# Layer 1's input projection: 41 more weight units in three fp32r products, 60 low parts made ahead in layer 0's FFN and read back from DRAM

## The reference, cut to what matters

```
xn = rmsnorm(x); proj = xn @ w_in                       # 2048 -> 8272 columns: u, q, k, v, index q/k/w, gates gl
q, k = rope(rmsnorm(.)); y_att = top-k sparse attention(q, k, v, index scores)
y_ssm = S5 scan(u) (complex states);  y_ssm = gelu(y_ssm); y_ssm *= sigmoid(y_ssm @ w_glu)
gates = sigmoid(gl)
x += (gates0 * (y_ssm @ w_branch0) + gates1 * (y_att @ w_branch1)) @ w_out
x += (silu(hn @ w_gate) * (hn @ w_up)) @ w_down         # hn = rmsnorm(x), width 5632
```

## Time and profile before

| | |
|---|---|
| median of 3 runs | 3007.73 us (3007.71 to 3008.23) |
| the profiled execution | 3008.11 us |
| its span | 3006.3 us |
| TensorE busy | 2963.9 us, 99% |
| VectorE busy | 1965.7 us, 65% |
| ScalarE busy | 1247.4 us, 41% |
| GpSimd busy | 254.5 us, 8% |
| granted TensorE clock | 1.00 of full speed |
| DMA | 546.45 MB, mean 182 GB/s |

### The profile page before, as it was taken

How to read it: one execution, slowest core, us unless ns; L and a number is a source line. 1 busy time by engine, 2 the same in 40 slices (tenths; PEclk the granted TensorE clock), 3 DMA queues, 4 the chain that set the end, 5 groups by cost and what they waited for, 6 DMA issues and landing times. The chain is left out here.

```text
span 3006.3 us, 58601 instructions
## 1 busy us (share of the span) xinstructions
PE 2963.9 (99%) x23480; PEld 2838.4 (94%) x23480; DVE 1965.7 (65%) x3145; ACT 1247.4 (41%) x1745; POOL 254.5 (8%) x239
## 2 busy tenths in 40 slices
PE   8999999999999999999999999999999999999999
PEld 7988888999999999999999887889999999999999
DVE  7669898577665545655576698985776555465653
ACT  4443234444545333334344423344444543333332
POOL 4420001300000000000034200013000000000000
PEclk9999999999999999999999999999999999999999
DMA  7547444655555655556555574456555555555564
GB/s 264 171 154 201 146 147 163 226 176 178 198 182 182 200 169 179 183 182 205 187 201 172 159 199 131 153 172 216 180 185 190 183 182 199 168 182 181 181 207 137
DMA packets 150623, 546.45 MB, mean 182 GB/s; under 512 B 19872, under 2 KB 25632, under 8 KB 149952
## 3 DMA queue, kind: packets, MB, share of 16 engines
q1 hardware_dynamic: 137728, 507.40, 50.4%
q0 software_dynamic: 12096, 35.67, 4.7%
q10 hardware_dynamic: 640, 1.16, 0.1%
HBM read 536.95 MB, written 7.21 MB: 181 GB/s over the span
## 5 line engine op out<-in xcount | busy, mean ns | idle before, releaser
L1847 DVE TENSOR_TENSOR w_ffn_low<-ring_ffn,w_ffn_high 128x1024 fp32r<-128x1024 f32 (+1 forms) x480 | 638.9, 1332 | 456.4 <-ACT w_ffn_high L1351 456.4
L1351 ACT ACTIVATE w_ffn_high<-ring_ffn 128x1024 fp32r<-128x1024 f32 (+1 forms) x480 | 548.1, 1142 | 641.6 <-PE main L1064 640.6
L1062 PE MATMUL main<-x_ffn_high,w_ffn_high 128*128 128x264 f32 x2816 | 791.7, 281 | 0.0
L1063 PE MATMUL main<-x_ffn_low,w_ffn_high 128*128 128x264 f32 x2816 | 791.3, 281 | 0.0
L1064 PE MATMUL main<-x_ffn_high,w_ffn_low 128*128 128x264 f32 x2816 | 791.3, 281 | 0.0
L1062 PEld LDWEIGHTS main<-x_ffn_high,w_ffn_high 128*128 128x128 f32 x2816 | 526.6, 187 | 0.1
L1063 PEld LDWEIGHTS main<-x_ffn_low,w_ffn_high 128*128 128x128 f32 x2816 | 526.6, 187 | 0.1
L1064 PEld LDWEIGHTS main<-x_ffn_high,w_ffn_low 128*128 128x128 f32 x2816 | 526.6, 187 | 0.0
L1062 PE MATMUL main<-hidden_high,w_ffn_high 128*128 128x264 f32 x1408 | 395.6, 281 | 0.0
L1063 PE MATMUL main<-hidden_low,w_ffn_high 128*128 128x264 f32 x1408 | 395.6, 281 | 0.0
L1064 PE MATMUL main<-hidden_high,w_ffn_low 128*128 128x264 f32 x1408 | 395.6, 281 | 0.0
(11 more groups left out here) (375 smaller groups left out, 4785.3 us busy)
## 6 DMA issues: line engine op xcount, KB each, us to landing
ring_ffn<-in_w_up SPq DMA_DIRECT2D x352, 512.0 KB, 3.3
ring<-in_w_in SPq DMA_DIRECT2D x260, 512.0 KB, 3.4
ring_ffn<-in_w_down SPq DMA_DIRECT2D x128, 704.0 KB, 4.1
ring<-in_w_br SPq DMA_DIRECT2D x64, 512.0 KB, 3.4
ring<-in_w_out SPq DMA_DIRECT2D x64, 512.0 KB, 3.3
w_low<-in_w_in POOLq DMA_DIRECT2D x20, 512.0 KB, 7.0
ring<-in_w_glu SPq DMA_DIRECT2D x16, 512.0 KB, 3.3
out_x<-x SPq DMA_DIRECT2D x7, 528.0 KB, 5.9
```

Source lines behind the costliest of these rows:

```text
L1062: mm(out, wfh[:, slot, w], high[:, kk, :], start=kk == 0, stop=False)
L1063: mm(out, wfh[:, slot, w], low[:, kk, :], start=False, stop=False)
L1351: af(wfh[:, s, 0:cols], ring_ffn[:, s, 0:cols], ACT.Copy).then_inc(high_ready, 1)
L1847: tt(wfl[:, s, 0:cols], ring_ffn[:, s, 0:cols], wfh[:, s, 0:cols].bitcast(F32), ALU.subtract).then_inc(low_ready, 1)
```

## The change

In layer 1 41 more units of `w_in` are split: 116 of 130 in place of 75, all from 65 on. 52 of them have their low part made by VectorE as before (`HALVED`), 4 by the accumulating DMA (`DRAWN`), and 60 get it from DRAM (`STORED`): there ScalarE still makes the high part in layer 1, while VectorE does nothing. These 60 low parts are made in layer 0's FFN, two in each of the 30 bodies (`beside`, after steps 2 and 6): GpSimd loads the raw unit of layer 1, ScalarE copies it to its fp32r rounding in `between` (the padding between the 264-wide rows of the FFN's moving operands), VectorE subtracts in place, GpSimd stores the result. Odd ones are held in two halves, the first of which lies over the last half slot of `ring`, so `prefetch(5)` waits until all odd ones are stored. In layer 1 SyncE loads a stored low part into `w_low` after its high part is made. The gates lie in `xn`'s place, the high parts get other places, x is reloaded 28 units later, the merged parts change places, and the units stand elsewhere: four more in the count stage, one fewer before the norms' spread, three in place of six in `s5_in(1)`. Layer 0's mixer is as it was.

```diff
-X_AT = 112
+X_AT = (112, 140)
+DRAWN = [60, 63, 66, 69]
+STORED = [67, 68, *(u for u in range(70, 132) if u not in (75, 79, 83, 87))]
+HALVED = [*range(10, 56), 59, 65, 75, 79, 83, 87, *range(G_GLU, G_END)]
+LOW_AT = {0: 59, 6: 65, 15: 75, 18: 79, 22: 83, 25: 87}
+HIGH_PLACE = {59: "b0", 60: "w2", 63: "w3", 65: "b0", 66: "w2", 67: "w1", 68: "w0", 69: "w3",
+              **{u: ("q0", "q1", "w2", "w3")[u % 4] for u in range(102, 118)},
+              **{u: ("e", "q0", "q1")[(u - 118) % 3] for u in range(118, 131)}, 131: "v"}
...
                 finish(i, s, up, half, n0, seq0)
+                if beside and s in (2, 6):
+                    beside(i, first_body, s // 4)
...
+            if layer and 56 <= u < G_GLU:
+                return max((n + 1 for n in (*HALVED, *STORED, *DRAWN) if n < u and high_place(n) == high_place(u)), default=0)
...
+                    def load_low(u):
+                        if layer and u in STORED:
+                            sp.wait_ge(unit_high, highs_by(layer, u))
+                            sp.dma_start(wlow[:, u % 6, :].bitcast(F32), d["lows"][STORED.index(u)]).then_inc(stored_low_in[u % 4], 16)
...
+                    def load_with_x(u):
+                        load(u)
+                        k = u - X_AT[layer]
+                        if 0 <= k < NT:
+                            sp.dma_start(x[:, k, :], (o["x"] if layer else d["x"])[:, k, :]).then_inc(x_in, 16)
+                        if u - 2 < 118:
+                            load_low(u - 2)
+                        if u - 3 >= 118:
+                            load_low(u - 3)
...
                                 for u in (4, 5, 2, 3, 6, 7):
+                                    if u == 5:
+                                        sp.wait_ge(next_low_out[1], 32 * (len(STORED) // 2))
                                     prefetch(u)
...
-                    for f in range(28, 44):
-                        for c in range(2):
-                            w_in_unit(f, c)
-                            pe.wait_ge(count_ready, 2 * (f - 28) + c + 1)
-                            mm(side[0][:, 0:2], same_seq_r[:], n_over_r[:], start=True, stop=True).then_inc(total_ready, 1)
+                    for n in range(32):
+                        fill(1)
+                        pe.wait_ge(count_ready, n + 1)
+                        mm(side[0][:, 0:2], same_seq_r[:], n_over_r[:], start=True, stop=True).then_inc(total_ready, 1)
+                        if layer and n in (12, 18, 24, 30):
+                            fill(1)
...
-                    fill(2)
+                    fill(1 if layer else 2)
...
-                    s5_in(1, 50, 6)
+                    s5_in(1, None, 3 if layer else 6)
...
+                            if layer:
+                                highs_to(2 * f + 5 if f < 57 else min(2 * f + 4, 130))
...
+                    if layer:
+                        act.wait_ge(v_out, 16)
+                        highs_to(131)
+                        act.wait_ge(units, 130)
                     gelu(0)
...
+                    def next_layer_high(i, first_body, odd):
+                        act.wait_ge(next_raw_in[odd], i * (16 + 16 * odd) + (16 + 16 * odd) * (first_body + 1))
+                        act.wait_ge(coming_low, i * 2 + (2 * first_body + odd + 1))
+                        if odd:
+                            af(between[:, 0:16, :], odd_first[:].bitcast(F32).rearrange("p (c n) -> p c n", n=32), ACT.Copy)
+                            af(between[:, 16:32, :], odd_last[:].bitcast(F32).rearrange("p (c n) -> p c n", n=32), ACT.Copy)\
+                                .then_inc(coming_high, 1)
+                        else:
+                            af(between, even_part[:].bitcast(F32).rearrange("p (c n) -> p c n", n=32), ACT.Copy).then_inc(coming_high, 1)
...
+                    def next_layer_low(i, first_body, odd):
+                        dve.wait_ge(coming_high, i * 2 + (2 * first_body + odd + 1))
+                        if odd:
+                            for part, at in ((odd_first, 0), (odd_last, 16)):
+                                raw = part[:].rearrange("p (c n) -> p c n", n=32)
+                                op = tt(raw, raw.bitcast(F32), between[:, at:at + 16, :].bitcast(F32), ALU.subtract)
+                            op.then_inc(coming_low, 1)
...
+                    if layer == 0:
+                        pool.wait_ge(units, UN_FFN)
+                        for n in range(2):
+                            next_raw(n)
+                        for n in range(len(STORED)):
+                            pool.wait_ge(coming_low, n + 2)
+                            store_low(n)
+                            pool.wait_ge(next_low_out[n % 2], (16 + 16 * (n % 2)) * (n // 2 + 1))
+                            if n + 2 < len(STORED):
+                                next_raw(n + 2)
```

More of the change, by code:

```diff
@@ L368, in high_free, with highs_by, lows_by, stored_by @@
             return u - 3
-        def highs_by(u):
-            return sum(n <= u for n in SPLIT)
-        def lows_by(u):
-            return sum(n <= u for n in SPLIT)
+        def highs_by(layer, u):
+            return sum(n <= u for n in high_made(layer))
+        def lows_by(layer, u):
+            return sum(n <= u for n in low_made(layer))
+        def stored_by(u):
+            return 16 * sum(n <= u and n % 4 == u % 4 for n in STORED)
         main = [ctx.enter_context(nc.psum_tensor(f"main{i}", [P, 512], F32)) for i in range(4)]
@@ L550, in build @@
         for layer in range(DEPTH):
+            made_high, made_low, added = high_made(layer), low_made(layer), low_by_adding(layer)
             with nc.Block() as block:
@@ L1094, in highs_to @@
                             next_high += 1
-                            if u not in SPLIT and u not in ADDED:
+                            if u not in made_high and u not in added:
                                 continue
-                            raw, high, low = unit_w(u)
+                            raw, high, low = unit_w(layer, u)
                             act.wait_ge(u_in[u % 6], landed(u))
-                            if high_free(u):
-                                act.wait_ge(units, high_free(u))
-                            if u in ADDED:
+                            if high_free(layer, u):
+                                act.wait_ge(units, high_free(layer, u))
+                            if u in added:
                                 af(high, raw, ACT.Copy)
@@ L1401, in lows_to @@
                             next_low += 1
-                            if u not in SPLIT:
+                            if u not in made_low:
                                 continue
-                            raw, high, low = unit_w(u)
-                            dve.wait_ge(unit_high, highs_by(u))
+                            raw, high, low = unit_w(layer, u)
+                            dve.wait_ge(unit_high, highs_by(layer, u))
                             tt(low, raw, high.bitcast(F32), ALU.subtract).then_inc(unit_low, 1)
@@ L1986, in _ @@
                     for b in range(3):
-                        pool.wait_ge(units, 2 * 63 + 2 * b)
+                        pool.wait_ge(units, 131 if layer and b else 2 * 63 + 2 * b)
                         gather_keys(b)
```

219 lines of the change are left out of this document (149 added, 70 removed).

## The result

The changed kernel takes 3022.71 us (median of 4 runs, 3018.09 to 3026.65) against 3007.72 for the kernel before on the same chip (3007.16 to 3008.23): a ratio of 1.005, 95% interval [1.0038, 1.0063]. It is 15 us slower, where 7 us faster was forecast and 3015 was the upper end of the range. The profiled execution took 3026.65 us, its span is 3024.8 us at a mean granted clock of 0.997; the kernel before had 1.000.

The account below looks back on a forecast made before the run. Bound: TensorE (busy 2963.9 of 3006.3 us), but with VectorE in layer 1's count and attention stages. Sum: -9.5 (`w_glu` earlier) + 2.7 (end of layer 0) = -6.8 on 3008.11, 3001.3, or 3001.0 for the median; range 2989 to 3015.

Parts of the forecast that it names:

- Stored low parts in layer 1: Layer 1's reads from DRAM: budget 8.0 us, 5.0 for units 118 to 130, landing 3.4 us, so no cost.
- From `w_glu` on the units are as before: Layer 1 from `w_glu` to its end: units unchanged, so no further difference in time.
- Count stage: Layer 1's count stage: 36 units in place of 32, 115.3 us, ending 4.4 us later.
- First softmax step: VectorE's first softmax step in layer 1: at 1896.4, 8.5 us earlier.
- Attention stage: Layer 1, first softmax step to scan's end: VectorE still needs 94.0 us, so the scan ends 8.5 us earlier.
- `w_glu`: Start of layer 1's `w_glu`: at 2002.9, 9.5 us earlier.
- Layer 0's FFN: Making two low parts in each body of layer 0's FFN fits the engines' and DMA's slack: cost nothing.
- End of layer 0: Unit 5's load waits for the last stores, landing after 4 to 7 us: cost 1.0 to 4.0, 2.7 taken.
- C: Rival: stored low parts late in layer 1's units 70 to 107, 32 units wait 1.0 us each: 3033, chance 0.08.
- A: Rival: TensorE stays the bound all through, gaining 27 less 2.7 us: 2984, chance 0.08.
- B: Rival: little left; count stage +5 or late second scan in layer 1, 4 us at layer's end: 3007, chance 0.24.
- D: Rival: layer 0's FFN stalls, 0.5 us in each of 30 bodies: 3016, chance 0.08.

Follow-up runs that it names:

- e10: Changed kernel without loads of stored low parts (high part taken twice, output wrong) and with e6's places for the merged values: 3001.62 us, ratio 0.9985.
- e6: Changed kernel with layer 1's merged values elsewhere: high part where the low part lay, low part in the free place: 3014.73 us.
- e4: Changed kernel without layer 1's loads of stored low parts; the high part is taken a second time instead, output differs: 3013.04 us.
- e1: The changed kernel run once more, unaltered, to see its spread: 3020.95 us (3018.63 to 3024.63).
- e3: Changed kernel with layer 1 as changed, but layer 0's FFN makes only two low parts, which every read takes: 3021.95 us.
- e8: Changed kernel with 58 stored low parts, not 60: units 67 and 68 stay fp32, none made in layer 0's last FFN body: 3025.56 us.
- e9: Changed kernel with TensorE held once, 1.68 us, between the first up and first down half of layer 1's FFN: 3021.91 us.
- e13: e12's order of issue (low part ahead of raw weights) with the changed kernel's own places for the merged values: 3035.23 us.
- e11: e6's kernel with low parts stored only for units 70 to 117; units 67, 68 and 118 to 131 fp32, output differs: 3004.82 us.
- e12: e6's kernel with SyncE issuing a unit's stored low part ahead of the raw weights, not behind them: 3022.85 us.
- e15: e6's kernel run once more, unaltered: 3015.4 us (3012.93 to 3022.61).
- e16: e6's kernel with a fourth place for the high parts of units 119 to 125, made one unit earlier, low-part loads likewise: 3017.32 us.
- e2: Only layer 0's half of the change: its FFN makes and stores the low parts, layer 1 as in the kernel before: 3009.54 us, ratio 1.0015.
- e5: Kernel before with TensorE held three times, 5.3 us each, in layer 1's `w_out`: 3030.82 us.
- e7: Kernel before with the places of the merged values' high and low part exchanged in layer 1: 3007.55 us, ratio 1.0001.
- e14: e2's kernel run once more, unaltered: 3009.81 us, six runs 3007.7 to 3010.9, two at 3018.0 and 3019.1.

## Why the prediction was wrong

**The step that failed first: "Stored low parts in layer 1 ... the cost as nothing".** It reckoned from the place: free three steps before the unit, 9.06 less 1.06 us, 8.0 us for the read, 5.0 for units 118 to 130. That ScalarE would be free to make the high part at that moment was never checked. In the attention stage its order puts the high parts behind copies that wait for TensorE, and there only three places are left. At the worst wait the read had, in place of 5.0 us, less than nothing: it was issued 1.06 us after TensorE was ready for the unit (1972.52 against 1971.46). The landing was mis-sized too (5.2 us in the middle, 3.4 taken), yet the worst wait had a landing of 3.4. Cost: 13 us, e10 against e6; 8 us, e4 against e1, with the other cause present. e6's profile has 11.4 us of waits for low parts and five stretches at half clock, e10's none and one; the runs do not separate what the waits cost from what the clock did, nor either from the loads' traffic, which e4 and e10 take away too.

**The second: "From `w_glu` on the units are as before".** The units' code is, their operands' places are not. With the change's places the products of `w_out` are 121.9 ns apart against 120.8, and layer 1's FFN runs at 121.3 against 120.0: 8.4 us. It was so in all 7 profiles with these places (after, e1, e3, e4, e8, e9, e13), in none of the 6 with e6's places (e6, e10, e11, e12, e15, e16) and in none of the 5 with those of before or their exchange (before, e2, e5, e7, e14). Cost: 8.4 us in the profiles of e4 and e10; by medians 6 to 11, e1 against e6 and e4 against e10. These places are shown to go with the pace; what in them does it is not known.

**The two together** are 19.3 us (e1 less e10), more than the 7.9 (e4) and 6.2 (e6) that each gives back alone. Whether one covers a part of the other, or the medians of 5 to 11 runs that spread over 6 to 15 us are off by that much, is not shown. Without them the kernel is at the forecast's time, if not with a right output.

The remaining steps can be read in e10, whose layer 1 began its split products 1.3 us later than before.
- *Count stage* +4.4: +5.0.
- *First softmax step* -8.5: 7.4 earlier, 8.7 against the start of layer 1.
- *Attention stage* 94.0: 94.0 (to the end of the scan's last operation).
- *`w_glu`* -9.5: 8.6 earlier, 9.9 against the start of layer 1.
- *Layer 0's FFN*, nothing: 0.4 us in the profile of after, 1.7 for all of this half in e2.
- *End of layer 0*, 1.0 to 4.0, 2.7 taken: 0.4.

At the end of layer 0 TensorE never waited for unit 5. After's rows, TensorE at the layer's end, then the landing of the last two stores:
```profile
1508.96 7.28 PE L507 MATMUL main<-arena,ring 128*128 128x264 f32 x32
1518.25 0.68 PE L780 MATMUL side<-rs,consts 128*128 128x264 f32 x2 [2.01 <-PEq L2165]
```
```profile
DMA to landing us min/median/max: 2.3/2.4/2.6
```
Units 4 and 5 take 7.28 us as in the earlier trace rows; what grew is the wait at the barrier behind them, from 1.57 to 2.01 us. The forecast had the stores land after 4 to 7 us; they were issued at 1505.11 and 1505.64, and unit 5's load could go out at 1508.25. In after six fp32 units behind that wait took 1.7 us more at half clock, which the forecast did not have, and which followed the same 2.0 us wait in 4 of 12 profiles.

So e10's agreement to 0.6 us is in part luck: the 2.3 us that were too many at the layer's end stand against 0.8 us of a later start of layer 0's FFN and 1.3 us that e10 loses between `w_glu` and the FFN (2234.36 against 2241.66 us at the FFN, 7.3 earlier, after 8.6 at `w_glu`).

**The rivals.** C named the right object, late stored lows, and the wrong place and price: units 70 to 107, one wait a unit. The trace has one such wait in the count stage and seven from unit 118 on, and what made the longest long was the late high part, not the 347 GB/s. That traffic is seen in the median landing, 5.2 us against 3.4. A did not happen: TensorE was not the bound in the attention stage even in e10. B's 5 us in the count stage came in part (after lost 6.7 there against 4.4, counted from the start of its split products). D did not happen as a stall.

The prediction weighed a rule of the Trainium skill against the rows ("DMA: Bandwidth & Descriptors", section "Anatomy of one DMA — SWDGE (gpsimd) path"): 2.0 us plus the bytes over 436 GB/s, 2.6 us for a half and 3.2 us for 512 KB. It set the rule aside, and at the layer's end that was wrong: the two halves landed in 2.3 and 2.6 us, and the trace agrees with the rule there. Beside the FFN's other traffic (288 GB/s in the window above) it does not: GpSimd's raw reads of 512 KB landed in 5.7 us and its stores in 4.4.

**Left open.** Why the places of the merged values, which the FFN does not read, go with its pace; why one program has either pace; and why a hold of 1.7 us did not change it in the profiled execution. The rows exclude the clock (1.00), waits (TensorE is busy all the time) and the load of VectorE and ScalarE (no busier). The second groups of e2, e10 and e11 are open too.

## What to carry to other kernels

When a transfer may only start after another engine's step, count its time from where that step stands in that engine's order, behind every wait ahead of it, and not from when its buffer is free. A wait of TensorE can cost more than its length, since the matmuls behind it may run at half clock: slack in a stage does not make late data free. A store's landing should be taken from a row of the same size and the same traffic: 7.0 us of an accumulating read of twice the size gave a term of 2.7 us where 0.4 was lost. And a kernel whose TensorE never stops should have the distance of its matmuls compared before and after, in a stretch that the change does not touch: 1.3 ns each was over half of this loss.

## What the hardware showed that I had not expected

- A hold of 5.3 us in `w_out` cost 7.8 us, with matmuls 0.22 us apart behind each of three (e5). The length of a shorter wait did not decide. The same wait of 2.0 us at the end of layer 0 was followed by half clock in 4 of 12 profiles (after, e1, e13, e14), one of 1.5 to 1.6 us there in none of 6 (before, e3, e5, e7, e8, e11); a wait of 2.11 us was followed by it in after, waits of 2.4 to 2.8 us between 2072 and 2088 us in e3, e4, e11 and e15 were not.
- Identical code with TensorE busy without a break has two steady paces, 120.0 and 121.3 ns for a 128x264 product (385 or 386, or 381 or 382 matmuls in 46 us), each kept through a whole FFN; layer 0's FFN was seen with both (after and e13). The eight units of layer 0's `w_glu`, too, stand at 121.3 ns in twelve profiles and at 120.9 in six (e2, e8, e13, e14, e15, e16).
- Several programs have two groups of times 8 to 10 us apart (e2: 3008.3 to 3009.6 and 3015.6 to 3019.3; e10: 2999.7 to 3003.0 and 3009.3 to 3010.4; e11: 3001.6 to 3005.1 and 3011.2 to 3017.0). An FFN at the longer pace would be 8.4 us; only e13's profile caught one such, so this reading is likely and not shown for the others.
